# First FFN of a two-block transformer kernel: seven block products instead of eight for two of the eight pairs of row blocks in the gate and up projections

## The reference

```python
h = rmsnorm(x, norm_ffn[l])
x = x + (jax.nn.silu(h @ w_gate[l]) * (h @ w_up[l])) @ w_down[l]
```

## Time and profile before

| | |
|---|---|
| median of 3 runs | 2469.32 us (2469.0 to 2469.39) |
| the profiled execution, its own time | 2469.4 us |
| its span, first to last instruction | 2467.7 us |
| PE busy | 2461.9 us |
| DVE, ACT, POOL busy | 1496.4, 1207.9, 626.7 us |
| TensorE clock granted | full, 1.00 of 2.4 GHz |
| moved by DMA | 511.70 MB, mean 207 GB/s |

### The profile page before, as it was taken

How to read it: one execution, slowest core, us unless ns; L and a number is a source line. 1 busy time by engine, 2 the same in 40 slices (tenths; PEclk the granted TensorE clock), 3 DMA queues, 4 the chain that set the end, 5 groups by cost and what they waited for, 6 DMA issues and landing times.

```text
span 2467.7 us, 30451 instructions
## 1 busy us (share of the span) xinstructions
PE 2461.9 (100%) x10976; PEld 2038.2 (83%) x10976; DVE 1496.4 (61%) x1723; ACT 1207.9 (49%) x1623; POOL 626.7 (25%) x537
## 2 busy tenths in 40 slices
PE   9999999999999999999999999999999999999999
PEld 7888888888888888888888888888888888888887
DVE  5766666555455555565455565576567647665665
ACT  6555445444344434455444544544555545553553
POOL 3665524210012100131011322332334103320330
PEclk9999999999999999999999999999999999999999
DMA  9888868776677667687667667777787767776775
GB/s 251 215 203 212 208 193 228 209 203 202 192 203 210 201 194 204 201 241 203 176 204 197 196 202 201 210 212 223 221 218 203 218 193 219 219 209 194 202 227 177
DMA packets 491587, 511.70 MB, mean 207 GB/s; under 512 B 187121, under 2 KB 290005, under 8 KB 491345
## 3 DMA queue, kind: packets, MB, share of 16 engines
q1 hardware_dynamic: 490112, 507.88, 73.2%
q0 software_dynamic: 1088, 2.07, 0.3%
q10 hardware_dynamic: 272, 0.26, 0.0%
HBM read 467.38 MB, written 2.11 MB: 190 GB/s over the span
## 4 chain that ended last, share of the span: by engine, by line
PE 53%; DMA 0%; DVE 0%; ACT 0%; POOL 0%; issue 0%
PE ps L617 17%; PE ps L619 17%; PE ps L618 17%; DMA raw<-in_w_in 0%; PE ps L954 0%; PE ps L715 0%; PE ps L700 0%; DVE w_lo L1417 0%; PE ps L934 0%; ACT w_hi L1021 0%; PE ps L889 0%; PE ps L888 0%; PE ps L725 0%; ACT z L1060 0%; POOL rstd L2151 0%
## 5 line engine op out<-in xcount | busy, mean ns | idle before, releaser
L1417 DVE TENSOR_TENSOR w_lo<-raw,w_hi 128x1024 fp32r<-128x1024 f32 x880 | 1152.2, 1312 | 924.2 <-ACT w_hi L1021 921.5
L1021 ACT ACTIVATE w_hi<-raw 128x1024 fp32r<-128x1024 f32 x879 | 929.4, 1059 | 1142.7 <-PE ps L619 1080.3
L617 PE MATMUL ps<-w_hi,xT_hi 128*128 128x512 f32 x2200 | 862.3, 392 | 0.3 <-ACT z L1060 0.2
L619 PE MATMUL ps<-w_hi,xT_lo 128*128 128x512 f32 x2200 | 856.7, 389 | 0.0
L618 PE MATMUL ps<-w_lo,xT_hi 128*128 128x512 f32 x2200 | 856.2, 389 | 0.0
L617 PE MATMUL ps<-w_hi,yT_hi 128*128 128x512 f32 x1312 | 511.4, 390 | 0.0
L619 PE MATMUL ps<-w_hi,yT_lo 128*128 128x512 f32 x1312 | 510.5, 389 | 0.0
L618 PE MATMUL ps<-w_lo,yT_hi 128*128 128x512 f32 x1312 | 510.5, 389 | 0.0
L617 PEld LDWEIGHTS ps<-w_hi,xT_hi 128*128 128x128 f32 x2200 | 413.0, 188 | 88.6 <-issue 2.5
L619 PEld LDWEIGHTS ps<-w_hi,xT_lo 128*128 128x128 f32 x2200 | 413.0, 188 | 86.0
L618 PEld LDWEIGHTS ps<-w_lo,xT_hi 128*128 128x128 f32 x2200 | 413.1, 188 | 85.2
(11 more groups left out here) (214 smaller groups left out, 923.2 us busy)
## 6 DMA issues: line engine op xcount, KB each, us to landing
raw<-in_w_up SPq DMA_DIRECT2D x264, 512.0 KB, 4.3
raw<-in_w_down SPq DMA_DIRECT2D x176, 512.0 KB, 4.6
raw<-in_w_in SPq DMA_DIRECT2D x160, 512.0 KB, 4.1
raw<-in_w_gate SPq DMA_DIRECT2D x88, 512.0 KB, 4.4
raw<-in_w_out SPq DMA_DIRECT2D x60, 512.0 KB, 4.7
raw<-in_w_in SPq DMA_DIRECT2D x128, 192.0 KB, 3.0
raw<-in_w_in SPq DMA_DIRECT2D x192, 128.0 KB, 2.8
raw<-in_w_proj_m SPq DMA_DIRECT2D x16, 512.0 KB, 4.3
```

The lines of the kernel that those rows point to most:

```text
L617: pe.matmul(o, hi[:, q], w_hi[n % NS][:, k, 0:width], start=first, stop=False)
L619: mm = pe.matmul(o, lo[:, q], w_hi[n % NS][:, k, 0:width], start=False, stop=last)
L1021: nc.scalar.activation(w_hi[n % NS][:, :, 0:width], raw[n % NS][:, :, 0:width], ACT.Copy).then_inc(hi_ready, 1)
L1417: v.tensor_tensor(w_lo[n % NS][:, :, 0:width], raw[n % NS][:, :, 0:width], f32(w_hi[n % NS][:, :, 0:width]), ALU.subtract).then_inc(lo_rea ...
```

## The change

For the first two pairs of row blocks of each group (`SUMMED_PAIRS = 2`), rows 0 to 255 and 256 to 511 of `w_gate` and `w_up`, the eight products of a block of x (two token tiles by two row blocks) with a block of weights (two row blocks by gate and up) are made by seven, after Winograd's form of Strassen's algorithm. Write x00, x10 for the first row block's tokens of tile 0 and 1, x01, x11 for the second's, g0, g1, u0, u1 for the two row blocks of gate and up.

- **Weight terms.** POOL makes four for each pair and group (`terms`), 128 x 512 each: `term_up` = u1 - u0, `term_first` = u0 - g0, `term_second` = `term_up` + g0, `term_crossed` = g1 - `term_second`. Each has one buffer; POOL waits for DVE's split of the same term of the pair before.
- **Parts.** The 48 matmuls of a pair's two units become four parts with 6, 6, 6 and 3: "first" (g0, `term_up`), "sums" (`term_first`, `term_second`), "crossed" (g1, `term_crossed`), "last" (u1). ACT and DVE split them half by half, each half 128 x 512, into the same four slots. They take banks 4 to 7 for the shared products, and banks 0, 1 and 2.
- **Sums of x.** POOL scales four tiles of x of 128 x 256 and makes four sums of 256 columns (`sum_x`), behind the first quarter's join; ACT and DVE split them (`xs_hi`, `xs_lo`, 128 x 1024) at step 3 of `out_a`'s second half.
- **Loads.** A pair's weights come by two loads of 512 KB into a buffer of its own (`load_pair`), both pairs' ahead of the group's first load.
- **Order of a group,** 20 units instead of 16: gate 2, first 0, sums 0, crossed 0, last 0, gate 3, the four parts of pair 1, gate 4 to 7, up 2 to 7. 186 matmuls instead of 192.
- **Putting together.** ACT copies bank 4 (`copy_shared`, step 10), DVE adds banks 5 to 7 with four instructions (`mix`, step 11), adds the gate banks with two (`gate_sum`, step 14); the tanh is at step 15, `gate` at 16, and `product`, at step 19, now has two additions ahead of its two multiplications.
- **Order elsewhere.** POOL does the terms of a group's two pairs ahead of turning the group before (behind it in the first group of a third), and the first group's between keeping and joining quarters 2 and 3. The transposes stand elsewhere in SP's queue. `x_hi` and `x_lo` of quarter 3 move to step 7. The Fori loops over a third's groups are written out. Some semaphores are merged.

```diff
+SUMMED_PAIRS = 2
+PARTS = ("first", "sums", "crossed", "last")
+ORDER = [("gate", 2), *((part_, 0) for part_ in PARTS), ("gate", 3), *((part_, 1) for part_ in PARTS),
+         *(("gate", u_) for u_ in range(4, 8)), *(("up", u_) for u_ in range(2, 8))]
...
+    def summed_groups():
+        return [GROUP_AT[k + 1] + 11 if k + 1 < GROUPS and FIRST_OF[k + 1] > 0 else GROUP_AT[k] + len(ORDER) - 1 + AHEAD for k in range(GROUPS)]
+    asked = [*quarters("out_a", 4, False)[:2], GROUP_AT[0], GROUP_AT[0] + ORDER.index(("gate", 3)), *summed_groups(), *quarters("ffn1_down2", 6, True), *quarters("proj_a", 4, False),
...
+            def load_pair(k, j):
+
+                if k == 0:
+                    sp.wait_ge(ha.y_lo, FREE + HEADS)
+                else:
+                    sp.wait_ge(lo_ready, NS + PART_AT[k - 1, j, "last"] + 1)
+                for e, w in enumerate((a["w_gate"][0], a["w_up"][0])):
+                    sp.dma_start(pair_raw[j][:, e, :, :], rows(w)[j][:, :, k * W:(k + 1) * W]).then_inc(pair_landed[j], 16)
...
+                    if kind == "first":
+                        if u == 0:
+                            pe.wait_ge(mixed_step, 5 * k)
+                            if k == 0:
+                                pe.wait_ge(ha.y_lo, FREE + HEADS)
+                                pe.wait_ge(x_sums_made, 10)
+                        product(4, xT, of_x(2 * u, 0), n, 0, done_)
+                        mm = product(7, xs, of_sums(u, 2), n, 1, done_)
+                    elif kind == "sums":
+                        product(5, xs, of_sums(u, 0), n, 0, done_)
+                        mm = product(6, xs, of_sums(u, 1), n, 1, done_)
+                    elif kind == "crossed":
+                        product(0, xT, of_x(2 * u + 1, 0), n, 0)
+                        mm = product(1, xT, of_x(2 * u + 1, 1), n, 1)
+                    elif kind == "last":
+                        if u == 0:
+                            pe.wait_ge(*evac_free(by_dve, up, BY_DVE, i, 1))
+                        mm = product(2, xs, of_sums(u, 3), n, 0)
...
+            def split_pair(n, k, j, part):
+
+                m = SUMMED_PAIRS * k + j
+                hi = w_hi[n % NS]
+                gate_, up_ = pair_raw[j][:, 0, :, :], pair_raw[j][:, 1, :, :]
+                act.wait_ge(slot_used, n + 1)
+                if part == "first":
+                    act.wait_ge(pair_landed[j], 32 * (k + 1))
+                    nc.scalar.activation(hi[:, 0, :], gate_[:, 0, :], ACT.Copy)
+                    act.wait_ge(terms_ready, 4 * m + 1)
+                    nc.scalar.activation(hi[:, 1, :], term_up, ACT.Copy).then_inc(hi_ready, 1)
...
+                dve.wait_ge(hi_ready, n + 1)
+                for c, src in enumerate(srcs):
+                    op = v.tensor_tensor(w_lo[n % NS][:, c, :], src, f32(w_hi[n % NS][:, c, :]), ALU.subtract)
+                op.then_inc(lo_ready, 1)
...
+                    def product(k, i):
 
                         dve.wait_ge(ffn_scale, 2)
...
+                        dve.wait_ge(mixed_step, 5 * (k + 1))
+                        dve.wait_ge(slot_used, NS + GROUP_AT[k] + len(ORDER))
                         for tt in range(NT):
...
+                            v.tensor_tensor(up_sum[:, tt, :], up_sum[:, tt, :], pair[1][tt][:], ALU.add).then_inc(by_dve, 1)
+                        dve.wait_ge(tok_made, 4 * k + 2)
+                        for tt in range(NT):
+                            dve.wait_ge(by_dve, FREE + PH[up][BY_DVE] + 4 * i + 3 + tt)
+                            v.scalar_tensor_tensor(tok_act[:, tt, :], tok_gate[:, tt, :], half_r_sq[:, tt:tt + 1], up_sum[:, tt, :],
+                                                   ALU.mult, ALU.mult).then_inc(tok_made, 1)
...
+                gate_, up_ = pair_raw[j][:, 0, :, :], pair_raw[j][:, 1, :, :]
+                pool.wait_ge(pair_landed[j], 32 * (k + 1))
+                free("first")
+                g_.tensor_tensor(term_up, up_[:, 1, :], up_[:, 0, :], ALU.subtract).then_inc(terms_ready, 1)
+                free("sums")
...
+                g_.tensor_tensor(term_first, up_[:, 0, :], gate_[:, 0, :], ALU.subtract).then_inc(terms_ready, 1)
+                pool.wait_ge(terms_ready, 4 * m + 1)
+                g_.tensor_tensor(term_second, term_up, gate_[:, 0, :], ALU.add).then_inc(terms_ready, 1)
+                free("crossed")
+                pool.wait_ge(terms_ready, 4 * m + 3)
+                g_.tensor_tensor(term_crossed, gate_[:, 1, :], term_second, ALU.subtract).then_inc(terms_ready, 1)
...
+            for k in range(1, GROUPS):
+                if FIRST_OF[k] == 0:
+                    turn_act(k - 1)
+                for j in range(SUMMED_PAIRS):
+                    terms(k, j)
+                if FIRST_OF[k] > 0:
+                    turn_act(k - 1)
+            turn_act(GROUPS - 1)
```

More of the change, by code:

```diff
@@ L165, with landed_in_slot @@
     LANDED.append(BY_SLOT[n_ % NS])
+def landed_in_slot(n):
+    return BY_SLOT[n % NS] + sum(m not in SUM_UNITS for m in range(N_SPLIT + (n - N_SPLIT) % NS, n + 1, NS))
 def heads_at(unit):
@@ L853, in ffn1 @@
                     up, down, n_fg, units = f"ffn1_up{t}", f"ffn1_down{t}", width // W, width // (UK * P)
-                    def up_turn(i, behind):
-                        for g in range(2):
-                            group(up, i, 16, g, 8, xT, 0, evac_free(by_dve, up, BY_DVE, i, g), ready=tiles_ready(KT), behind=behind)
-                    up_turn(0, nothing)
-                    with pe.Fori(1, n_fg) as i:
-                        up_turn(i, nothing)
+                    for i in range(n_fg):
+                        up_group(fg0 + i, up, i)
                     def act_ready(u):
@@ L2103, in landed, with turn_x @@
                 pool.wait_ge(across, 32 * (k + 1))
-            def turn_x(name, base, kept=True, ahead_of_last=None):
+            def turn_x(name, base, kept=True, ahead=nothing, behind=nothing):
                 for q in QUARTERS:
@@ L2116, in turn_x @@
                         g_.tensor_copy(x[:, :, q * W:(q + 1) * W], fresh[q % 2]).then_inc(x_kept, 1)
-                    if q == 3 and ahead_of_last:
-                        ahead_of_last()
+                    ahead(q)
                     landed(TURNS[name] + q)
@@ L2123, in _, with first_terms, first_sums @@
+            def first_terms(q):
+                if q >= 2:
+                    terms(0, q - 2)
+            def first_sums(q):
+                if q == 0:
+                    sum_x()
             pool.wait_ge(ha.y_lo, FREE + HEADS)
-            turn_x("out_a", KT)
+            turn_x("out_a", KT, ahead=first_terms, behind=first_sums)
             pool.wait_ge(ss_ready, 1)
```

310 lines of the change are left out of this document (217 added, 93 removed).

## The result

The changed kernel takes 2527.41 us (median of 4, 2525.26 to 2529.65) against 2469.36 before: ratio 1.0235, 95% interval 1.0218 to 1.0253. The direction was forecast, the size (2488, range to 2505) was not. Busy times and slices of the page, after; compare.

What follows compares the result with a forecast made beforehand. PE was taken as the bound, busy for 2461.9 of 2467.7 us. Matmuls removed -15.0, steady groups +18.4, first group +15 gave +18.4 us, forecast 2488 us; own range 2475 to 2503, with the other cases 2466 to 2505.

Steps and rivals of the forecast that it cites:

- What the change removes: First FFN: 48 of 192 matmuls become 42 in each group, 1.36 us a group, 15.0 us over 11 groups.
- A matmul that comes late costs its whole delay: PE, busy for 2461.9 of 2467.7 us at full clock: a late matmul costs its whole delay.
- Both cases cost more than 1.36 ... I take 2.3: Eight steady groups: DVE and POOL sharing the port costs 2.3 us each, 18.4 us in all (ends 9 and 28).
- POOL gets its turn in DVE's gaps: Steady group: POOL's terms and copies make last 0 0.9 us late, gate 3 1.4 later still; 2.3 us, up to 3.0.
- my list: DVE's work in a steady group from PE's start on gate 2; without POOL, PE never waits, with 0.4 us left.
- a rival: Shared port becomes the bound; slower bursts of the pair loads could tip it over, 4 to 5 us a group; chance 0.08.
- The second case: Steady group: DVE keeps the port, POOL's copies wait, gate 6's load comes late behind SP's transposes; 1.8 to 2.8 us.
- A term of POOL: Each two-input POOL operation of 128x512 was taken at 1.23 us, with ends 1.04 and 1.31.
- The first group: Group 0: sums of x and pair loads delay gate 2 by 7.5 us, gate 3 and 4 by 7.5; 15 us, ends 5 and 18.
- Groups 4 and 8: These groups follow a down phase, with two additions instead of product and copies: nothing added.
- The port as the bound: Rival: DVE and POOL fill the shared port, 41.4 of 42.16 us a group; if tipped over, 2506 to 2512 us; chance 0.08.
- three signs that I named for being wrong: Steady groups of 42.2 us, gate 2's load issued before 383, or DVE and POOL overlapping undisturbed would refute the forecast.

Runs made afterwards that it cites:

- e14: Changed kernel with one summed pair instead of two, order and pair loads moved, scalings of x on ACT, additions behind the second quarter's halves: 2471.9 us.
- e5: Kernel before the change, with the first FFN's up loops of PE, ACT and DVE written out: 2469.4 us.
- e12: Kernel before the change, first FFN's DVE loop written out, three extra DVE instructions delaying DVE once in each of 11 up groups: 2479.3 us.
- e10: Changed kernel without POOL's terms, and with POOL's halves and joins of the first FFN's activations cut to 1/32 of their width: 2480.0 us.
- e13: Changed kernel with pair loads made for group 0 only; later groups use group 0's blocks again: 2522.4 us.
- e2: Changed kernel in which POOL makes no terms; ACT and DVE split plain weight blocks in their place: 2490.5 us.

## Why the prediction was wrong

- **What the change removes**, 15.0 us: right. The matmuls outside the slow stretches keep their 0.2267 us, in units of three and six too (e14's 42.84). Written-out loops cost nothing (e5).
- **"A matmul that comes late costs its whole delay"** is the step that failed most. It cost its delay and, behind the longer waits, a stretch at half speed: 20.9 us that stand nowhere in my sum, which put the clock at nothing. The trace of before, at the full clock in each slice, could not show it; the granted clock of the changed kernel does (0.50 for 51.2 us, PE busy for 41.75 of them), and e12 shows that waits of 0.7 us and less do not bring it about.
- **"Both cases cost more than 1.36 ... I take 2.3"** a steady group, 18.4 us: too small. Less group 0's 16.3 us (48.60 - 32.28), PE idles 28.5 us more than before, nearly all of it in the eight steady groups: 3.6 each. With what is counted as busy and with the slow clock, a steady group takes 48.4 us on average, 6.2 over 42.16. The case "POOL gets its turn in DVE's gaps" was the right one, with its waits at last 0 and gate 3, but my list starts at t = 0 with gate 2, first 0 and sums 0 split. In the trace DVE had just begun the half splits then. The additions start at 4.8 instead of 3.6, the multiplications end at 8.4 instead of 6.2, last 0 is ready at 9.9 instead of 7.7. Two things put it there: gate 2's load lands 8.44 us after its issue (3.9 in the earlier trace rows), which I had only as part of a rival, and POOL's terms draw out the splits of first 0 and sums 0 as well. Of the two the terms are the larger: without them the waits before last 0 go, without the pair loads 9.0 of 21.9 us stay. The second case, a late load of gate 6 behind the transposes, shows in e10 and e13 rather than here (0.9 us in all at gate 6).
- **A term of POOL**, 1.23 us: 1.29 alone, within its ends.
- **The first group**, 15 us: close as a sum of idle time (16.3), but by luck, with gate 2 at 10.2 instead of 7.5 and gate 3 at 5.9 instead of 7.5 with gate 4. The slow clock adds some 5 us there (PE at half speed for 9.5). The scalings, for which I had no row, were mis-sized (4.6 us for 1.6); the load was issued at 389.98 instead of 387.5 and landed at 397.7 instead of 395; and 2.1 us more are x's second quarter, whose tiles stand behind gate 2's split and are in no term of mine (gate 2 was split at 400.1, PE started at 402.15).
- **Groups 4 and 8**: right, with 42.56 and 42.16 us.
- **The port as the bound** had 0.08. It gives the best account of the waits, though no run isolates it as a sum: with two pairs no order and no placing of the loads brought the group under 47 us, with four terms and seven half splits fewer all waits went. Its 2506 to 2512 us had no clock in it either, and with 4 to 5 us in eight groups the sum comes to 2501 to 2509. It is no pure sum of port time, though: by the prediction's durations e2 has less on the port than e14 (31.6 against 34.7 us) and still waits. That its nine short units stand close together would explain this, but is not shown. How much of the 47 us is the port's sum and how much the short stretch, these runs leave open; e13's growing waits at gate 6 are also not taken apart further.

None of the three signs that I named for being wrong came: steady groups of 42.2 us, a load issued before 383, undisturbed overlap. All three guard against a change that costs less than forecast; none looks at the clock.

Forecast +18.4, measured +56.2 in the span: of the difference of 37.8, 20.9 are the clock's, 5.5 the part of the waits that is counted as busy, 10.1 idle time of the steady groups and 1.3 of the first.

## What to carry to other kernels

When one engine is busy all the time, price a stall with what follows it: here 44.8 us of listed idle time went with 20.9 us of slow clock and 5.5 us of waiting that is counted as busy, while short waits alone (e12) had the last part only. To tell them apart, read the granted clock and not just the busy time. Before fewer matmuls are bought with work on DVE and POOL, write down both engines' lists for the stretch where units get short, from before its start, and count what they share; being four units ahead was 5 us of slack with long units and 0.4 with short ones, by the prediction's lists. Try the change at half its size and leave out the phase that is already crowded: one pair from the second group on won 5 us where two pairs lost 58.

## What was unexpected of the hardware

- In the steady groups PE's clock fell to its lower level behind pairs of waits of which no single one was over 3.3 us: behind 3.0 and 1.0 us seven matmuls ran at a pitch of 0.43 us. 11 single waits of at most 0.7 us left it at 1.00 (e12). In e13, 0.9 and 1.0 us brought it down once, and did not in another group.
- A growth of busy time is not a slower clock by itself: 0.3 us of each wait is counted as busy.
- A scaling of 128x256 by a column on POOL took 0.92 us at the least and 1.16 in the mean of four, more than half of a two-input operation of twice its width (1.29).
- Removing all pair loads, 2 MB a group, made the steady groups only 1.1 us shorter (e13): a transfer in the way is a place where slack is lost, and the slack was missing anyway.
